# Padding on-chip tiles, regrouping sparse attention's keys, queries and values, and moving the modulation rows in a two-block hybrid and expert kernel

## The reference, cut to what matters

```
kc = compress(to_g(partial_rope(kv(nkc), cos, sin)), cmp_pos_k, cmp_w1_k, cmp_w2_k)
vc = compress(to_g(kv(nvc)), cmp_pos_v, cmp_w1_v, cmp_w2_v)
ks, kw = rope of nks, nkw;  vs, vw = nvs, nvw
p_c, p_s, p_w = masked softmax of q against kc, ks, kw
y_nsa = g0 * (p_c @ vc) + g1 * (p_s @ vs) + g2 * (p_w @ vw)       # per head
compress: blocks of 32 tokens, flattened to 2048, gelu(flat @ w1) @ w2
```

## Time and profile before

| | |
|---|---|
| Median of 3 runs | 2392.18 us (2391.69 to 2393.94) |
| Profiled execution | 2398.61 us, span of the core's instructions 2396.8 us |
| PE busy | 2130.4 us, 89% of the span |
| DVE busy | 1472.9 us, 61% |
| ACT busy | 1045.1 us, 44% |
| DMA | 371.73 MB, mean 155 GB/s |

### The profile page before, as it was taken

One profiled execution on the slowest core, in us unless ns is written; L12 is line 12 of the kernel. 1 busy time (PEld: TensorE's weight loads), 2 busy tenths in 40 slices (PEclk: granted clock), 3 DMA queues, 4 the chain that ended last, 5 costly groups with the idle time before them and its releaser, 6 DMA issues. The chain is left out here.

```text
span 2396.8 us, 40348 instructions
## 1 busy us (share of the span) xinstructions
PE 2130.4 (89%) x16970; PEld 2022.8 (84%) x16970; DVE 1472.9 (61%) x2373; ACT 1045.1 (44%) x1465; POOL 0.2 (0%) x4
## 2 busy tenths in 40 slices
PE   6879888999979787989996687999979898899997
PEld 5878867999978777889995677999979877799997
DVE  3757555687868564657876555555548654465554
ACT  3643434454355433435442334444446553344443
POOL 0000000000000000000000000000000000000000
PEclk9889888999989887989998888999989998899999
DMA  4333322588944233235887313555525321355552
GB/s 152 124 114 106 115 75 94 170 304 301 321 143 133 89 106 106 89 128 199 323 307 261 132 61 106 174 180 177 176 88 169 131 79 54 123 167 176 179 176 95
DMA packets 101269, 371.73 MB, mean 155 GB/s; under 512 B 11489, under 2 KB 11745, under 8 KB 100705
## 3 DMA queue, kind: packets, MB, share of 16 engines
q1 hardware_dynamic: 99936, 364.78, 45.1%
q10 hardware_dynamic: 1152, 4.38, 0.5%
HBM read 368.07 MB, written 1.05 MB: 154 GB/s over the span
## 5 line engine op out<-in xcount | busy, mean ns | idle before, releaser
L293 DVE TENSOR_TENSOR low<-raw,high 128x1024 fp32r<-128x1024 f32 x594 | 725.3, 1223 | 492.6 <-ACT high L290 489.5
L290 ACT CAST high<-raw 128x1024 fp32r<-128x1024 f32 x594 | 618.4, 1046 | 577.0 <-PE ps L358 554.5
L356 PE MATMUL ps<-hh,high 128*128 128x256 f32 x2864 | 838.2, 293 | 26.3 <-PEq L589 11.2
L357 PE MATMUL ps<-hh,low 128*128 128x256 f32 x2864 | 823.3, 287 | 0.0
L358 PE MATMUL ps<-hl,high 128*128 128x256 f32 x2864 | 822.1, 287 | 0.0
L356 PEld LDWEIGHTS ps<-hh,high 128*128 128x128 f32 x2864 | 560.6, 196 | 45.4 <-issue 38.4
L357 PEld LDWEIGHTS ps<-hh,low 128*128 128x128 f32 x2864 | 561.0, 196 | 0.5 <-issue 0.5
L358 PEld LDWEIGHTS ps<-hl,high 128*128 128x128 f32 x2864 | 559.4, 195 | 0.0
L356 PE MATMUL ps<-ffn_high,high 128*128 128x256 f32 x672 | 190.0, 283 | 3.8 <-DVE ffn_low L1864 2.4
L357 PE MATMUL ps<-ffn_high,low 128*128 128x256 f32 x672 | 187.5, 279 | 0.0
L358 PE MATMUL ps<-ffn_low,high 128*128 128x256 f32 x672 | 187.4, 279 | 0.0
(11 more groups left out here) (427 smaller groups left out, 2898.0 us busy)
## 6 DMA issues: line engine op xcount, KB each, us to landing
raw<-in_stream SPq DMA_DIRECT2D x594, 512.0 KB, 3.4
ada_rows<-in_ada SPq DMA_DIRECT2D x96, 512.0 KB, 5.3
bias<-in_bias ACTq DMA_DIRECT2D x1, 1536.0 KB, 6.0
xT<-in_xT ACTq DMA_DIRECT2D x1, 1024.0 KB, 6.5
c_act<-in_c SPq DMA_DIRECT2D x2, 512.0 KB, 5.1
out<-xT SPq DMA_DIRECT2D x1, 1024.0 KB, 3.9
par<-in_par SPq DMA_DIRECT2D x1, 858.0 KB, 4.7
hybrid_const<-in_const ACTq DMA_DIRECT2D x1, 800.0 KB, 5.6
```

The source lines that it names most:

```text
L290: return act.copy(self.high[:, slot, :], self.raw[:, slot, :])
L293: return dve.tensor_tensor(self.low[:, slot, :], self.raw[:, slot, :], self.high[:, slot, :].bitcast(F32), ALU.subtract)
L356: pe.matmul(out, sh, mh, start=start, stop=False, **more)
L357: pe.matmul(out, sl, mh, start=False, stop=False, **more)
```

## The change

1. `sb` follows every on-chip tile whose size, rounded up to 32 bytes, is no multiple of 64 bytes with a filler, so that the next one starts at a multiple of 64.
2. The first block's start: x is loaded in four pieces on SP's queue, the first two ahead of the first unit; ahead of them only the norm's gains (8 columns) are asked for on ACT's queue, the other parameters later. PE runs unit 1 ahead of the sums of squares and unit 2 ahead of the spreading of the scale; ACT and DVE have their chunks of x ahead of units 1 to 3.
3. Queries are laid out by group (`group_query`: group 0 in partitions 0 to 63), so the keys stand once: `nks` and `nkw` (4 units per layer) become `nkk` (2 units), `qk` has 8 tiles, `rope` has 4 steps, GLA's plan has one pair less.
4. `compress` multiplies by 256 columns in both matmuls (`wide`; the columns beyond 64 or 32 are neighbours' values that nobody reads); two small copies on ACT give the last ones defined values.
5. `values`: the turned probabilities (128 columns) are stationary and the values (64 columns) move, so the result lies by token; at the end ACT copies two banks to `W`, PE turns 8 squares of 128x128 over, and ACT and DVE split as before.
6. `Modulation`: 24 rows in each SwiGLU's gate and up units as before, none in its down units; the other 48 in the first mixture (`mixture(0)`), about 0.6 rows per unit from its unit 12 on. `modulated_gains(0)` shares a block with the sums of squares, `modulated_gains(1)` is at the end of that mixture. In `Entry.vector` a chunk's last unit comes behind `split` instead of ahead of it.

The diff, cut to its core:

```
+    parts = {n: feature(cols(n)) for n in ("hf", "hq", "gq", "gk", "hog", "gog")}
+    parts.update({n: feature(twice(n)) for n in ("nkc", "nvc")})
+    by_group = cols("nq").reshape(D, NSA_G, NSA_H // NSA_G, NSA_DH).transpose(0, 2, 1, 3).reshape(D, NSA_H * NSA_DH)
+    parts.update({"nq": feature(by_group), "nkk": feature(np.concatenate([cols("nks"), cols("nkw")], axis=1))})
...
+            tile = scope.enter_context(nc.sbuf_tensor(name, shape, dt))
+            short = -((4 * math.prod(shape[1:]) + 31) // 32 * 32) % LINE
+            if short:
+                scope.enter_context(nc.sbuf_tensor("after_" + name, [P, short // 4], F32))
+            return tile
...
+            for c in range(KD // 2):
+                sp.dma_start(xT[:, 2 * c:2 * c + 2, :], x_in[:, 2 * c:2 * c + 2, :]).then_inc(x_loaded[c], 16)
+                if c == 1:
+                    ring.load(sp, 0, 0)
+            for i in range(1, RING):
                 ring.load(sp, i, i)
             for i in range(RING):
                 sp.wait_ge(ring.split.sem, i + 1)
...
-            act.dma_start(xT[:, :, :], x_in).then_inc(x_loaded, 16)
-            for l in range(DEPTH):
-                act.dma_start(par1[:, l, :], par1_in[l, :, :]).then_inc(x_loaded, 16)
+            act.dma_start(par1[:, 0, 0:KD], par1_in[0, :, 0:KD]).then_inc(gains_loaded, 16)
             act.dma_start(const[:, :], const_in[:, 0:N_KEPT]).then_inc(loaded, 16)
             act.dma_start(lb[:, :], lb_in).then_inc(loaded, 16)
...
                 if res is None:
+                    product(pe, 0, u, 1, None)
                     pe.wait_ge(loaded, 16 * 2)
-                    for c in range(KD // 2 - 1):
+                    for c in range(KD // 2):
                         self.add_sums(pe, c)
-                self.add_sums(pe, KD // 2 - 1)
-                product(pe, 0, u, 1, None)
-                self.spread(pe)
-                for j in range(1, EARLY):
+                    product(pe, 1, u, 0, None)
+                    self.spread(pe)
+                    product(pe, 1, u, 1, None)
+                else:
+                    self.add_sums(pe, KD // 2 - 1)
+                    product(pe, 0, u, 1, None)
+                    self.spread(pe)
+                    product(pe, 1, u, None, None)
+                for j in range(2, EARLY):
                     product(pe, j, u, None, None)
...
+                    self.round(act, 0)
+                    first_round(act, 0)
+                    for j in range(1, KD // 2):
+                        self.round(act, j)
+                    first_round(act, 1)
+                    for j in range(KD // 2):
+                        square_tiles(act, j)
+                    for j in range(2, RING):
                         first_round(act, j)
...
+                if res is None:
+                    dve.wait_ge(gains_loaded, 16)
+                    dve.wait_ge(x_loaded[0], 16)
+                    self.weigh(dve, 0)
+                    dve.wait_ge(x_loaded[1], 16)
+                    self.weigh(dve, 1)
+                    self.split(dve, 0)
+                    first_split(dve, 0)
+                    for j in range(2, KD // 2):
+                        dve.wait_ge(x_loaded[j], 16)
+                        self.weigh(dve, j)
+                        self.split(dve, j - 1)
+                    self.split(dve, KD // 2 - 1)
+                    for j in range(1, RING):
                         first_split(dve, j)
-                        if j == 0:
-                            dve.wait_ge(x_loaded, 16 * (1 + DEPTH))
+                    bounds_differences(dve)
...
                     self.weigh(dve, j)
-                    if res is not None:
-                        res.unit(dve, units[-1])
                     self.split(dve, j)
-                if res is None:
-                    bounds_differences(dve)
-                if res is not None and res.mods is not None:
-                    res.mods.finish(dve)
+                    res.unit(dve, units[-1])
...
+            at = j * 2 * (2 * NCMP + 2)
+            return flat((fh, fl)[i][:, 12:22, :])[:, at:at + T]
...
                 def _(pe):
-                    for j in range(5):
-                        if j == 4:
...
-                            pe.matmul(ps[:, 4 + i, 0:2 * cols], wh, both[i][:, j, :], start=(j == 0), stop=False,
-                                      skip_group_check=True)
-                            ins = pe.matmul(ps[:, 4 + i, 0:cols], wl, both[i][:, j, 0:cols], start=False,
-                                            stop=(j == 2 * BLOCKS - 1), skip_group_check=True)
+                            pe.matmul(ps[:, 4 + i, 0:T], wh, wide(i, j), start=(j == 0), stop=False)
+                            ins = pe.matmul(ps[:, 4 + i, 0:T], wl, wide(i, j), start=False, stop=(j == 2 * BLOCKS - 1))
...
+                        act.copy(flat((fh, fl)[i][:, 12:22, :])[:, 16 * 2 * cols:16 * 2 * cols + n], W[:, i, 0:n])
...
+            lo = h // 4 * NSA_DH
+            return qk[lo:lo + NSA_DH, h % 4, t * P:(t + 1) * P]
...
+                g, c32 = h // 4, 32 * (h % 4)
                 pe.wait_ge(pt_ready.sem, pt_ready.base + i + 1)
                 for t in range(TT):
-                    o = ps[lo:lo + NSA_DH, h // 4, h // 2 % 2 * T + t * P:h // 2 % 2 * T + (t + 1) * P]
-                    pe.matmul(o, vcm[c32:c32 + NCMP, g * NSA_DH:(g + 1) * NSA_DH],
-                              ptc[c32:c32 + NCMP, 2 * t + h // 4, :], start=True, stop=False, tile_position=(c32, lo))
+                    o = ps[:, t, h * NSA_DH:(h + 1) * NSA_DH]
+                    pe.matmul(o, ptc[c32:c32 + NCMP, 2 * t + h // 4, :], vcm[c32:c32 + NCMP, g * NSA_DH:(g + 1) * NSA_DH],
+                              start=True, stop=False, tile_position=(c32, 0))
                     for b in range(2):
                         for s in range(t + 1):
-                            ins = pe.matmul(o, vsw[:, s, b * P + g * NSA_DH:b * P + (g + 1) * NSA_DH],
-                                            turned(2 * h + b)[:, (t + s) * P:(t + s + 1) * P], start=False,
+                            ins = pe.matmul(o, turned(2 * h + b)[:, (t + s) * P:(t + s + 1) * P],
+                                            vsw[:, s, b * P + g * NSA_DH:b * P + (g + 1) * NSA_DH], start=False,
                                             stop=(b == 1 and s == t))
                 tell(ins, pv_done)
+                if h == NSA_H - 1:
+                    for t in range(TT):
+                        pe.wait_ge(by_token.sem, by_token.base + t + 1)
+                    for m in range(4):
+                        for t in range(TT):
+                            at = m % 2 * T + t * P
+                            ins = pe.transpose(ps[:, m // 2, at:at + P], W[:, 1, t * BANK + m * P:t * BANK + (m + 1) * P],
+                                               ident)
+                        if m % 2:
+                            tell(ins, by_feature)
             def act_after(act, i):
                 if 4 <= i < 2 * NSA_H:
                     act.wait_ge(pv_done.sem, pv_done.base + (i - 4) // 2 + 1)
                 if i == 2 * NSA_H:
                     act.wait_ge(pv_done.sem, pv_done.base + NSA_H)
+                    for t in range(TT):
+                        tell(act.copy(W[:, 1, t * BANK:(t + 1) * BANK], ps[:, t, :]), by_token)
                     for m in range(2):
-                        ins = act.copy(flat(yh[:, 2, 2 * m:2 * m + 2, :]), ps[:, m, :])
-                    tell(ins, to_dve2)
+                        act.wait_ge(by_feature.sem, by_feature.base + m + 1)
+                        tell(act.copy(flat(yh[:, 2, 2 * m:2 * m + 2, :]), ps[:, m, :]), to_dve2)
...
+                    dve.wait_ge(ada_full[i % 2], 16 * (row // 2 + 1))
                     r = self.rows[:, i % 2, :]
                     dve.scalar_tensor_tensor(r, r, 1.0, self.c[:, :], ALU.mult, ALU.mult,
-                                             accum_out=self.now[:, i:i + 1]).then_inc(ada_used.sem, ada_used.one())
+                                             accum_out=mod[:, row // ADA, row % ADA:row % ADA + 1]) \
...
+                             [[(0, None)], [(1, 0)], [(1, 1)], [(2, 0)], [(2, 1)], [], [], [], [(3, None)]], 1)
             assert proj.mine.stop == len(proj.pairs)
...
+            down = Residual(22, KF, (fh, fl))
...
+            mods = Modulation(DEPTH, ADA, ADA, moe) if l == 0 else None
+            def rows(i):
+                return min(max((i - 11) * ADA // 80, 0), ADA)
             with new_block() as block:
                 @block.sync
                 def _(sp):
-                    w.sync(sp)
+                    for i in range(w.n):
+                        w.sync(sp, [i])
+                        if mods is not None:
+                            mods.sync(sp, rows(i))
                 @block.tensor
...
+                        if s >= LAG and mods is not None:
```

(32 more changed lines are left out.)

138 lines of the change are left out of this document (51 added, 87 removed).

## The result

The changed kernel takes 2369.17 us, median of 4 runs (2367.49 to 2369.75), beside 2393.06 for the kernel before (2391.69 to 2397.58): ratio 0.9896, 95% interval 0.9879 to 0.9913. It is faster by 24 us, not by the 73 I forecast, and lies outside my range. Its profiled execution took 2368.76 us with a span of 2367.0.

A forecast was written before the change was run, and what follows sets the result against it. PE, busy 89% of the span, was taken to bound the kernel: matmul count times pace in long stages, plus holes elsewhere. Terms summed to -72.6 us, from median 2392.2 to 2319.6 us; range 2282 to 2350.

The forecast's parts named there:

- 1, pace: Matmuls moving hh or hl, 8400 of them, follow each other faster once aligned: -21 us, between 3 and 38 us gained.
- 2, start: First block: first matmul near 9 us instead of 15.51, block ends at 50 or 51: -15 us, ends -9 and -19.
- 6, down products: Ends of both SwiGLU down products, without modulation rows: -13.5 and -11.5 us, together -25, ends -18 and -28.
- 6, first mixture: First mixture takes the 48 modulation rows, 59 us of DVE work: +1 us, ends 0 and +10.
- 3, GLA: Two GLA steps lose their matmuls and shrink by 3 us at most: -1.5 us per layer, -3, ends +2 and -6.
- 3, rope: Rope has one step fewer of five at 1.4 us: -1.1 us per layer, -2.2 in all.
- 4, compression: Compression's 64 matmuls per layer, all wide, keep the clock: -1.3 us per layer, -2.6, ends +0.5 and -3.5.
- 5, values by token: Sparse attention: -0.52 us per head, +2.1 at the block's end; -2.1 per layer, -4.2, ends +4 and -8.
- my fourth rival: First mixture: SP's waits for used rows delay units' loads and PE waits for each; slower by 90 us; chance 0.02.
- Covered: First mixture: loads up to 5.7 us late, taking 3.4, hidden by issue 11 us ahead of ACT.
- Upper bound: no gain: Sparse attention's heads: the worst end for the new values form, against the forecast -0.52 us per head.
- My first rival: Whole kernel: alignment gives nothing, the rest comes as forecast, 2337 to 2341 us; chance 0.22.

The follow-up runs named there:

- e_line32: Changed kernel with its part 1 undone (LINE 32 instead of 64, tiles without fillers): 2356.0 us, ratio 0.9841.
- e_blocks: Changed kernel with compressed-score heads alternating between partition halves, GLA's single units in every second step, and compression narrow again: 2359.4 us.
- e_values: Changed kernel with part 5 undone (values stationary, probabilities moving, nothing turned back at the end): 2361.2 us.
- the first probe: Products-only kernel, 20 blocks of 240 matmuls, other engines idle, moving tiles and weights at varied places: 113.3 to 120.0 ns per matmul.
- the second: Products-only kernel, 47 blocks of 120 matmuls, varied places and interruptions: at 64 nine blocks 113.3 ns, five 117.8; at 192 all fourteen 117.8.
- e_best: Changed kernel with all moving tiles at place 64, compressed-score heads alternating between partition halves, and part 5 undone: 2320.0 us, ratio 0.9681.

## Why the prediction was wrong

The prices of parts 2 to 6 without the pace are read from e_line32, where hh has its old pace, as lengths of blocks in the traces.

| Step | Forecast | Measured | Read from |
|---|---|---|---|
| 1, pace | -21 | +13.2 | changed kernel less e_line32 |
| 2, start | -15 | -14.7 | 65.84 to 51.10 |
| 6, down products | -25 | -29.2 | 301.4 to 286.1 and 271.3 to 257.3 |
| 6, first mixture | +1 | +2.9 | 304.1 to 307.0 |
| 6, gains | -0.6 | -0.6 | 25.3 to 24.7 in the changed kernel |
| 3, GLA | -3 | +1.5 | 56.1 and 56.0 to 56.7 and 56.8 |
| 3, rope | -2.2 | -3.4 | 18.7 to 17.0, twice |
| 3, compressed scores | none | +2.1 | 20.7 to 21.8, twice |
| 4, compression | -2.6 | 0 | e_blocks |
| 5, values by token | -4.2 | +4.3 | changed kernel less e_values, blocks |

They add up to -23.9, and so do the medians. That agreement is luck: the traces of the two kernels differ by 29.8 us and not by 23.9, and blocks not in the table differ by up to 5 us from trace to trace with the clock (layer 1's HGRN with `prepare_gla`: 89.5 in the changed kernel, 84.4 in e_blocks).

**The step that failed** is part 1's: "If all go to the slower pace, 8400 x 0.4 ns = 3 us; if all to the faster, 8400 x 4.5 = 38 us ... so I take the middle, 21 us". Both ends had the wrong sign for what happened. I split the streams into those at a multiple of 64 and one that was not, and took the first group's two paces as the only ones an aligned tile can have. None of the aligned streams of before lay at the weights' own place; hh was moved exactly there, and 120.0 stood in no row. The table of addresses, written modulo 256 with the weights in it, would have shown that hh went to a place of which no row spoke, and the range should have had a loss in it. This alone is 34 of the 49 us. That a stream can have two paces was right, and that a wait can come with a change; but only at some places.

**Right:** the start, nearly to the microsecond, with PE at 10.56 instead of 9 us and the sums done at 18.29 + 3.71 = 22.0 as taken; the down products, 4 us better than forecast, with no wait of PE over 0.81 us left between the matmuls of those stretches. (The -11.7 us of layer 0 in that term comes out of no sum; the row gives a hole of 11.35.)

**Mis-sized:** rope by 1; the mixture's rows by 2. There my fourth rival had the right mechanism and the wrong size: SP's waits for used rows do make the units' loads late, and ACT waited 38.3 us for them, one of the signs of being wrong that the prediction named; but the lead of 11 us kept nearly all of it from PE. Of the 2.9 us, in the trace of e_line32, 0.86 are PE's wait for a low part, 1.1 the sums of squares behind it, which took 6.21 us instead of 5.10, and the rest isn't traced. "Covered" was nearly so. **Part 3 in GLA:** "the two steps shrink by 3 us at most" took DVE's 3.6 us as time for two steps; DVE was still behind with the units of the steps before (1.22 us each), so PE's matmuls in those steps had covered DVE's work and their removal left a hole and a half clock. The compressed scores, which the new layout of the queries touches too, I left out of the parts. **Part 4:** PE ended earlier but DVE's low parts were the cover I didn't name. **Part 5:** the end grew by 2.1 us as forecast. The gain per head came from GLA's spread at 112 ns and "fewer moving columns can't be slower"; most starts of the values are 111 or 112 ns apart indeed, but seven of sixteen are 160 to 205, where it was eight before, and 0.06 us is what was left of 0.52. "Upper bound: no gain" was the true end. One count was off without effect: part 3 removes 96 matmuls, not 192, since hh's went from 2864 to 2832 of each kind.

My first rival came closest (alignment gives no gain), but it had no loss in it, and its 2337 to 2341 would have needed parts 3 to 5 as forecast. The Trainium skill's page SBUF — State Buffer, section Operand start alignment, on which it leaned, gives a rule of what is allowed, not of speed. The runs don't test that rule, as every start here was at a multiple of the element size; they show that where an allowed operand starts is worth 113.3 to 120.0 ns per matmul.

## What to carry to other kernels

Write the start addresses of weights and moving operands modulo 256 before and after an edit of the layout; in a stage bound by matmuls, 64 bytes ahead of the weights' place beat the weights' own place by 39 us of 2369, and aligning by itself cost 13. A matmul that is taken away, or narrowed, pays only where no other engine has work queued behind the same step. A load that waits for its buffer goes on a queue of its own, not ahead of loads that could start: in the one kernel where it was tried that gave a stage of 300 us 4 back.

## What the runs showed of the hardware

- A stream of float32r products with 256 moving columns has a pace that depends on the places of weights and moving tile modulo 256 bytes, with nothing else running: 113.3 to 120.0 ns. The Trainium skill's page TensorE: Matmul & The Clock Gate, section Back-to-back issue gap, has 109 ns for this width by its formula, which it gives for a matmul by itself and not for a stream; no stream of this width here reached it.
- At place 64 with the weights at 128 the stream has two paces, 113.3 and 117.8 ns, and keeps one until it is interrupted. An even number of inserted matmuls in full float32 changed it in 63 of 64 cases, an odd number kept it in 52 of 56. Place 192 showed both paces as well (113.3 in the first probe, 117.8 in the second). Why is open: no counter of the profile shows it.
- The pace of a stretch differs between executions of one program, with 4.2 us in one block of e_best; the two executions were on different chips.
- Small matmuls (64 rows, 15 moving columns) at a granted clock of 0.50: 32 of them took 3.60 us when neighbours lay in different halves of the partitions, 4.49 when they lay in the same half.
